# A two-layer decoder trunk on one core: one more part of a pair's weights goes into the first norm's room, projection 9 goes ahead of the second turn, and step 5's maxima ahead of step 4's sums

## What is computed

```python
x = layer_norm(ALPHA * x + token_mixing(x))
x = layer_norm(ALPHA * x + moe(x))
```

```python
y = sum over the 8 chosen experts of gate * (silu(x @ w_gate) * (x @ w_up)) @ w_down
y = y + shared_expert(x)
```

## Time and profile before

| | |
|---|---|
| median of three runs | 1281.73 us (1280.99 to 1284.18) |
| the profiled execution's own time | 1279.44 us |
| its span | 1277.6 us |
| TensorE busy | 1236.9 us (97%) |
| VectorE busy | 550.9 us (43%) |
| ScalarE busy | 339.8 us (27%) |
| GpSimd busy | 132.6 us (10%) |
| DMA, mean over the span | 356 GB/s, 454.40 MB |

### The profile page before, as it was taken

How to read it: one execution, slowest core, us unless ns; L and a number is a source line. 1 busy time by engine, 2 the same in 40 slices (tenths; PEclk the granted TensorE clock), 3 DMA queues, 4 the chain that set the end, 5 groups by cost and what they waited for, 6 DMA issues and landing times.

```text
span 1277.6 us, 26853 instructions
## 1 busy us (share of the span) xinstructions
PE 1236.9 (97%) x10642; PEld 644.8 (50%) x10642; DVE 550.9 (43%) x1477; ACT 339.8 (27%) x700; POOL 132.6 (10%) x181
## 2 busy tenths in 40 slices
PE   9999989999999999999999999899999999999994
PEld 7885844334344344433398768433433444433431
DVE  4787553323332223332558875432332233233334
ACT  4667311111111111111246573111111111111111
POOL 2652310000000000000025433000000000000000
PEclk9998999999999999999999999999999999999998
DMA  8444779999999999999934438799999999999994
GB/s 350 166 170 194 270 284 421 421 422 422 422 421 420 421 420 421 422 421 421 391 127 179 190 140 337 290 420 421 421 422 422 421 420 420 421 420 421 422 422 189
DMA packets 63998, 454.40 MB, mean 356 GB/s; under 512 B 7472, under 2 KB 8112, under 8 KB 9904
## 3 DMA queue, kind: packets, MB, share of 16 engines
q1 hardware_dynamic: 63632, 452.23, 86.4%
q10 hardware_dynamic: 288, 1.05, 0.2%
HBM read 452.21 MB, written 1.05 MB: 355 GB/s over the span
## 4 chain that ended last, share of the span: by engine, by line
PE 80%; DVE 9%; ACT 4%; DMA 4%; issue 2%; SPq 1%; DVEq 0%; ACTq 0%; POOL 0%; POOLq 0%
PE banks L947 33%; PE banks L967 17%; PE banks L923 7%; PE banks L981 5%; DMA expert_weights<-in_moe_w 4%; PE banks L955 2%; PE banks L875 2%; PE banks L819 1%; ACT prob L1200 1%; PE banks L729 1%; PE banks L820 1%; PE banks L821 1%; PE banks L722 1%; PE banks L546 1%; PE banks L904 1%
## 5 line engine op out<-in xcount | busy, mean ns | idle before, releaser
L947 PE MATMUL banks<-expert_weights,gathered 128*64 128x512 f32 x2032 | 451.9, 596 | 4.5 <-DMA expert_weights<-in_moe_w 2.4
L947 PEld LDWEIGHTS banks<-expert_weights,gathered 128*64 128x64 f32 x2032 | 139.5, 137 | 312.4 <-issue 298.0
L967 PE MATMUL banks<-expert_weights,hT 128*32 128x512 f32 x2048 | 233.0, 595 | 2.2 <-DVE gathered L1709 1.1
L1722 DVE TENSOR_TENSOR sig<-sig,banks 128x256 f32<-128x256 f32 x64 | 26.9, 421 | 341.5 <-ACT sig L1293 341.2
L1303 ACT ACTIVATE y_hi<-banks,gate_slot 128x512 fp32r<-128x512 f32 x128 | 88.0, 687 | 309.1 <-PE banks L967 309.1
L1732 DVE SCALAR_TENSOR_TENSOR y_lo<-banks,gate_slot,y_hi 128x512 fp32r<-128x512 f32 x128 | 96.1, 750 | 169.5 <-ACT y_hi L1303 169.5
L1293 ACT ACTIVATE sig<-banks 128x256 f32<-128x256 f32 x64 | 24.5, 383 | 412.0 <-PE banks L947 412.0
L967 PEld LDWEIGHTS banks<-expert_weights,hT 128*32 128x32 f32 x2048 | 60.2, 109 | 139.6 <-issue 136.3
L923 PEld LDWEIGHTS banks<-hot,x_part 128*128 128x128 bf16 x3072 | 93.1, 98 | 50.9 <-issue 50.7
L923 PE MATMUL banks<-hot,x_part 128*128 128x64 bf16 x3072 | 100.7, 193 | 1.8 <-DVE hot L1704 1.8
L1356 POOL TENSOR_TENSOR piece_lo<-piece,piece_hi 128x256 fp32r<-128x256 f32 x112 | 84.5, 791 | 72.9 <-ACT piece_hi L1143 72.2
(11 more groups left out here) (211 smaller groups left out, 1296.8 us busy)
## 6 DMA issues: line engine op xcount, KB each, us to landing
expert_weights<-in_moe_w SPq DMA_DIRECT2D x382, 1024.0 KB, 17.7
piece<-in_pieces SPq DMA_DIRECT2D x32, 1024.0 KB, 5.0
shared_weights<-in_ws SPq DMA_DIRECT2D x2, 3072.0 KB, 12.3
ln_rows<-in_lnw SPq DMA_DIRECT2D x4, 1024.0 KB, 16.2
first_quarter_ahead<-in_moe_w SPq DMA_DIRECT2D x2, 1024.0 KB, 10.3
xT<-in_x_t SPq DMA_DIRECT2D x2, 512.0 KB, 6.3
piece<-in_first ACTq DMA_DIRECT2D x2, 512.0 KB, 6.8
x_sb<-in_x SPq DMA_DIRECT2D x1, 1024.0 KB, 16.0
```

The lines of the kernel that those rows point to most:

```text
L947: mm = pe.matmul(C[e * PAIR:(e + 1) * PAIR, :], xgT[:, d, e * PAIR:(e + 1) * PAIR], w[:, e, part], start=(d == 0), stop=(d == KD - 1))
L967: mm = pe.matmul((A, B)[c][to:to + SLOTS, :], hT[:, f, of_:of_ + SLOTS], W[:, QUARTERS + c, e, f * 512:(f + 1) * 512], start=(f == 0), sto ...
L1722: own.link(V.tensor_tensor(sig[:, :], sig[:, :], C[:, 0:EF], ALU.mult))
```

## The change

- **Weights.** Part 1 of pair 2 is loaded into the room of the norm's rows, `lnp`, as soon as both halves of the first norm are done (`normalised`). So part 1 of pair 4 goes straight behind part 0 of pair 4, once TensorE has read pair 0's part 1, and the refills of pairs 2 and 4 begin with part 2. TensorE reads the pair's first two parts from `ahead` and `lnp`. The second norm's rows wait until TensorE has read pair 2's gate and up parts; they still stand behind all weights in SP's list.
- **TensorE.** `project_tile(9, 0)` moves ahead of `turn_probs(1)` and `cmp_kv`, the first half of `project_tile(9, 1)` ahead of `add_values(1)` and the heads of projection 8, its second half ahead of `scores(2)`; `scores(4)` moves ahead of `add_values(2)`. At the start of layer 1, 12 matmuls on zeros take the place of the last 16.
- **ScalarE.** In layer 1 alone the cast of piece 5 moves ahead of `read_plain(2)`. In both layers the second half of the last cast moves from behind `read_turned(10)` to behind turn 7, which is behind the exps of units 5 and 6.
- **VectorE.** Both halves of `rotate(9)` stand ahead of `maxima(2)`; `maxima(5)` stands ahead of `normalise(4)`, not behind it.

```diff
-        gu_ld = [[sem(..., 16 * PAIRS // 2 - 16 * (q == 0 and s == 0)) for s in range(2)] for q in range(QUARTERS)]
-        ahead_ld = sem("quarter_ahead_loaded", 16)
+        gu_ld = [[sem(..., 16 * PAIRS // 2 - 16 * (q < 2 and s == 0)) for s in range(2)] for q in range(QUARTERS)]
+        ahead_ld = [sem(f"quarter{q}_ahead_loaded", 16) for q in range(2)]
...
-                    sp.wait_ge(*at(main.gu, 1))
-                    load_chunk(0, 0, 4)
-                    refill(0, 2, range(1, CHUNKS))
+                    for t in range(TT):
+                        normalised(sp, 0, t)
+                    sp.dma_start(lnp[:, :, :], chunk(2, 1)).then_inc(ahead_ld[1], 16)
+                    for q in range(2):
+                        sp.wait_ge(*at(main.gu, q + 1))
+                        load_chunk(0, q, 4)
+                    refill(0, 2, range(2, CHUNKS))
                     refill(1, 3)
-                    refill(0, 4, range(1, CHUNKS))
+                    refill(0, 4, range(2, CHUNKS))
                     refill(1, 5)
...
-                    for t in range(TT):
-                        normalised(sp, 0, t)
+                    sp.wait_ge(*at(main.gu, 3 * QUARTERS))
                     sp.dma_start(lnp[:, :, :].rearrange("p a d -> p (a d)"),
...
-                        keep_clock(16)
+                        keep_clock(12)
...
+                    project_tile(9, 0)
                     turn_probs(1)
                     cmp_kv()
-                    project_tile(9, 0)
+                    front, back = range(KD // 2), range(KD // 2, KD)
+                    project_tile(9, 1, front)
                     add_values(1)
                     turn_heads(8)
-                    front, back = range(KD // 2), range(KD // 2, KD)
-                    project_tile(9, 1, front)
+                    project_tile(9, 1, back)
                     scores(2)
-                    project_tile(9, 1, back)
...
+                    scores(4)
                     add_values(2)
-                    scores(4)
...
-                            w = W[:, q] if first_quarter is None or q else first_quarter
+                            w = held[q] if q < len(held) else W[:, q]
...
-                        if from_ahead:
-                            quarters[0] = (ahead_ld, 16)
-                        elif s == 0 and not first:
-                            quarters[0] = (gu_ld[0][0], 16 * i)
+                        for q in range(2):
+                            if from_ahead:
+                                quarters[q] = (ahead_ld[q], 16)
+                            elif s == 0 and not first:
+                                quarters[q] = (gu_ld[q][0], 16 * i)
...
                     split_hi(4)
+                    if layer:
+                        split_hi(5)
                     read_plain(2)
                     read_turned(1)
-                    split_hi(5)
+                    if not layer:
+                        split_hi(5)
...
-                    split_last_hi(1)
                     for v, (what, u) in list(enumerate(TURNS))[5:]:
                         if what == "unit" and u + 1 < NU:
                             exps(u + 1)
                         probs_out(v)
                         heads_out(v - 1)
+                        if v == 7:
+                            split_last_hi(1)
...
-                    rotate(9, (0,))
+                    rotate(9)
                     maxima(2)
-                    rotate(9, (1,))
...
+                    maxima(5)
                     for u in range(4, NU):
                         normalise(u)
...
-                        if u == 4:
-                            maxima(5)
```

More of the change, by code:

```diff
@@ L261, in build @@
         piece_ld = [sem(f"piece_loaded{s}", 16 * len(range(s or RING, len(STREAM), RING))) for s in range(RING)]
-        gu_ld = [[sem(f"gate_up_quarter{q}_loaded{s}", 16 * PAIRS // 2 - 16 * (q == 0 and s == 0)) for s in range(2)] for q in range(QUARTERS)]
-        ahead_ld = sem("quarter_ahead_loaded", 16)
+        gu_ld = [[sem(f"gate_up_quarter{q}_loaded{s}", 16 * PAIRS // 2 - 16 * (q < 2 and s == 0)) for s in range(2)] for q in range(QUARTERS)]
+        ahead_ld = [sem(f"quarter{q}_ahead_loaded", 16) for q in range(2)]
         dn_ld = [[sem(f"down_half{c}_loaded{s}", 16 * PAIRS // 2) for s in range(2)] for c in range(HALVES)]
@@ L455, in _ @@
                     sp.wait_ge(*at(proj, 2 * N_IN_PIECES))
-                    sp.dma_start(ahead[:, :, :], chunk(2, 0)).then_inc(ahead_ld, 16)
+                    sp.dma_start(ahead[:, :, :], chunk(2, 0)).then_inc(ahead_ld[0], 16)
                     sp.wait_ge(*at(o_sb, 8))
@@ L935, in turn_slots, with gate_up @@
                         mm.then_inc(sw.gts, 1)
-                    def gate_up(sw, W, k, loaded=None, first_quarter=None):
+                    def gate_up(sw, W, k, loaded=None, held=()):
                         pe.wait_ge(*at(sw.xg, 2 * k))
@@ L992, in step @@
                         quarters = [(gu_ld[q][s], 16 * i + 16) for q in range(QUARTERS)]
-                        if from_ahead:
-                            quarters[0] = (ahead_ld, 16)
-                        elif s == 0 and not first:
-                            quarters[0] = (gu_ld[0][0], 16 * i)
-                        gate_up(main, ex[s], n + 1, loaded=quarters, first_quarter=ahead if from_ahead else None)
+                        for q in range(2):
[3 more added lines that the diff above has]
+                                quarters[q] = (gu_ld[q][0], 16 * i)
+                        gate_up(main, ex[s], n + 1, loaded=quarters, held=(ahead, lnp) if from_ahead else ())
                         if first:
```

## The result

The changed kernel takes 1288.15 us, the median of five runs (1283.86 to 1289.19), against 1281.73 before. The ratio is 1.0041 with a 95% interval of 1.0024 to 1.0059: 5.3 us slower, between 3.1 and 7.6. I had said 1284.0, within 1277.8 to 1289.0. So the sign holds, the range holds by 0.9 us, and the size, 2.3 us, is less than half of the measured one. The 1281.5 to 1286 that I gave my own forecast is missed.

What follows compares the result with a forecast made beforehand. TensorE and DMA were both taken as near their limit in the experts, step order as deciding the mixing. -2.4 + 1.9 + 3.1 - 1.5 + 1.2 = +2.3 us on the 1281.73 median gave 1284.0, range 1277.8 to 1289.

Steps and rivals of the forecast that it cites:

- the mixing with the clock: Token mixing: +1.9 us in layer 0, +3.1 in layer 1, and 1.2 for new clock drops in both together.
- Weights, -2.4: Experts of both layers: part 1 fetched in idle DMA time saves 1.2 us a layer, bounds -0.2 and -3.8 for both.
- The fear that the queue has too little outstanding: DMA queue near 210 us: it may run dry and lose the weights' gain; as a rival 1286.2 us, chance 0.12.
- The last pairs: End of each layer's experts: excess of 1.98 and 2.67 us falls to 0.8 and 1.5; keeping the old values refutes.
- Projection 9 ahead of the second turn: Token mixer, both layers: turn of unit 1 4.1 us late, exps of unit 2 at 93.4, scores of unit 3 3.7 late.
- The wait that grows rather than being filled: TensorE ahead of projection 9: the wait of 1.44 us grows to about 2.4, released by VectorE's rotation.
- The tail: Mixing, units 4 to 7: moving the cast gives 1.5 us back, later sums cost 0.4, the cast put back 1.2.
- The start of layer 1, -1.5: Fewer matmuls on zeros give -0.6 us, the early cast ahead of the relu -0.9; bounds 0 and -1.5.
- The clock, the failed step: TensorE in mixing: old drop's end gives 2.5 us in layer 0, 1.2 less in layer 1; new drops cost 1.2, bounds 0 to 6.3.
- My second rival, a long drop in both layers: The 2.4 us wait drops the clock for 6.3 us in each layer: +7.4, 1289.1 us, chance 0.18.

Runs made afterwards that it cites:

- e1: The kernel before with the weights part alone (part 1 of the third pair held in the norm's room): 1280.74 us, ratio 0.9994 (0.9984 to 1.0003).
- e4: The kernel before with scores(4), maxima(5) and the second half cast moved as in the change, nothing else: 1281.78 us, ratio 0.9998.
- e11: The kernel before with 12 for 16 matmuls on zeros and the cast of piece 5 early in layer 1: 1278.81 us, ratio 0.9965.
- e3: The kernel before with projection 9 ahead of the second turn and its whole rotation ahead of unit 2's maxima: 1292.83 us, ratio 1.0089.
- e8: The kernel before, unchanged, run again for a second profile: 1280.61 us, one run.
- e6: The changed kernel with 18 matmuls on zeros in each new TensorE wait, ahead of projection 9 and unit 3's scores: 1283.38 us, 1.0011 of before.
- e7: The changed kernel with ScalarE's cast of the output piece ahead of the copy of unit 1's turned probabilities: 1280.35 us, 0.9987 of before.
- e12: The changed kernel, unaltered, run again for a second profile: 1288.51 us, 1.0040 of before (1.0024 to 1.0056).

## Why the prediction held, and where its sum was off

The ratios of the parts run alone add up: -0.8 for e1, -0.3 for e4, -4.5 for e11 and +11.4 for e3 make +5.9, and the whole measures +5.3. What I had for the same parts was -2.4 for the weights, -1.5 for the start of layer 1 and +6.2 for the mixing with the clock.

- **Weights, -2.4.** 2.0 in both layers by the mean of the profiles, 0.8 (2.1 faster to 0.4 slower) by e1's ratio: the sign is likely, not certain. The fear that the queue has too little outstanding was right, and cost more than half of the 4.9 us (two parts of 2.46) that were moved into the idle stretch. The last pairs speak against me as I had put it: I was to be wrong if they kept 1.98 and 2.67, and in the first profile they kept 2.90 and 2.72 (three intervals over 13.80). They were a poor mark, because the single profile of before had been a short one: e8 has 3.63 and 3.38 there. At the 416 GB/s that I named, a pair takes 15.1 us and not 14.9; nothing in the sum hangs on it.
- **Projection 9 ahead of the second turn.** The wait that grows rather than being filled, the late turn, the late cast, the standing difference and the late maxima came one after the other as forecast, and e6 has each within 0.3 us. e7 adds what I hadn't seen: had the cast been early, the second half of the rotation would still have held up the maxima, and only 1.8 us of the delay would have gone.
- **The tail.** The wait of 1.94 us did close. That this brings little was right; e4 puts it at nothing.
- **The start of layer 1, -1.5.** Measured 1.9 in the stretches, of which 0.67 is the turn of the rows (5.79 late at the last sigmoid, 5.12 at the turn; 0.6 forecast). e11's ratio gives 4.5, which the stretches don't explain.
- **The clock, the failed step.** I credited 2.5 and 1.3 us for the drops of before that would go, and charged 1.2 for new ones: net -2.6 with their 0.6 of waits left out. Measured, the low time rose from 6.8 or 10.2 us to 20.4. At half speed the 10.2 to 13.6 more are worth 5.1 to 6.8 us at most; the filled waits of e6 won 4.8. The page "TensorE: Matmul & The Clock Gate" of the Trainium skill (its terms) puts the penalty at the low time multiplied by the share of the clock that is taken away, and the runs here agree with that as an upper end. My error was in the count: I let the 2.4 us wait drop the clock once in the two layers, and didn't price the wait ahead of unit 3's scores at all, though the 3.7 us of delay there were in my own sum. My second rival, a long drop in both layers, gave 1289.1 and came closest; I had it at 0.18. Its number is partly luck as well: behind the wait ahead of projection 9 the clock was low for 3.4 us in each layer, not 6.3, and the rest of the low time came elsewhere.

With the clock's term at +5 in place of -2.6 the sum would have been 9.9 us, which is what the two first profiles differ by (9.8). Against the medians it would have been some 4 too high: the profiled execution of the changed kernel lay 1.0 above its median, and the one of before 2.3 below. e6 checks the rest of the sum without the clock, since its low time is that of e8: the terms other than the clock's make +4.9, and e6 is 1.4 us over before (0.1 to 2.6). So the rest was some 3 us too high while the clock's term was 7.6 too low, and that 2.3 came as near to 5.3 as it did is in part luck: two errors stood against each other. Which of the other terms was too high stays open; the profiles have the late steps as forecast, and e11's large gain points to the start of layer 1.

## What to carry to other kernels

Before work is put into an engine's wait, see what this work itself waits for: here it was released after the thing it was put ahead of, so the wait grew and everything behind the old step moved. Where TensorE gains new waits of 1 us and more, price a drop of its clock for each of them, though it may come at another place, and take two profiles of the same kernel before a difference of 1 or 2 us is read from a pair. A part that is held ahead of its time pays off where the queue has work behind it, not at the first chance.

## What the hardware showed that I had not expected

- The clock's drops aren't a fixed answer to a wait. Three of them began with or right behind a wait of only 0.42 to 0.44 us ahead of the turn of projection 9's heads (changed kernel 732.8, e12 93.2, e6 726.6). The wait of 1.94 us ahead of unit 7's scores was followed by 6.8 us at 1.2 GHz in the first profile of before, by 3.4 in e8 and by none in e1; one of 1.23 us (113.35) was followed by 3.4 in the changed kernel, and one of the same length by none in e4's layer 0.
- With few transfers outstanding the rate falls to 246 and 242 GB/s while the DMA engines' share is still 0.92 and 0.77 (two profiles of the changed kernel), and single 8 KB packets there take up to 1.4 and 1.6 us for 0.31. Why they do stays open.
